# Three norms of a fused transformer kernel: who adds the eight squared chunks, VectorE or TensorE

## The reference, cut to what matters

```python
def rmsnorm(x, g):
    x32 = x.astype(jnp.float32)
    y = x32 * lax.rsqrt(jnp.mean(x32 * x32, axis=-1, keepdims=True) + RMS_EPS)
    return y.astype(x.dtype) * g

for i in range(DEPTH):
    h = h + 0.5 * swiglu(rmsnorm(h, ffn_norm_a[i]), ...)
    m = rmsnorm(h, mix_norm[i])
    h = h + mixer(m, ...)
    h = h + 0.5 * swiglu(rmsnorm(h, ffn_norm_b[i]), ...)
```

## Time and profile before

| what | before |
|---|---|
| median of 3 runs | 1870.84 us (1870.21 to 1872.37) |
| the profiled execution's own time | 1869.32 us |
| its span, first to last instruction | 1867.5 us |
| TensorE matmuls busy | 1738.5 us (93%) |
| VectorE busy | 1274.3 us (68%) |
| ScalarE busy | 910.5 us (49%) |
| GpSimd busy | 320.8 us (17%) |

### The profile page before, as it was taken

How to read it: one execution, slowest core, us unless ns; L and a number is a source line. 1 busy time by engine, 2 the same in 40 slices (tenths; PEclk the granted TensorE clock), 3 DMA queues, 4 the chain that set the end, 5 groups by cost and what they waited for, 6 DMA issues and landing times.

```text
span 1867.5 us, 29197 instructions
## 1 busy us (share of the span) xinstructions
PE 1738.5 (93%) x11150; PEld 1378.9 (74%) x11150; DVE 1274.3 (68%) x2524; ACT 910.5 (49%) x1905; POOL 320.8 (17%) x335
## 2 busy tenths in 40 slices
PE   9999999999999999999999999999987787877777
PEld 8999979999999999689999899975532222322222
DVE  6555787555765575876566887896777776766454
ACT  5344665444544453764444565635444444344433
POOL 1000004000000000030000000444333333333332
PEclk9999999999999999999999999999999999999999
DMA  8555426965465545225555444699999999999998
GB/s 300 190 183 188 146 85 161 271 251 187 158 201 184 187 154 184 80 93 188 195 175 176 150 137 137 222 406 422 421 421 422 421 421 422 421 421 422 421 422 318
DMA packets 96138, 483.70 MB, mean 259 GB/s; under 512 B 10576, under 2 KB 10832, under 8 KB 63360
## 3 DMA queue, kind: packets, MB, share of 16 engines
q0 software_dynamic: 38976, 275.25, 38.2%
q1 hardware_dynamic: 57024, 206.59, 32.9%
HBM read 477.34 MB, written 4.46 MB: 258 GB/s over the span
## 4 chain that ended last, share of the span: by engine, by line
PE 59%; DMA 16%; DVE 10%; issue 8%; POOL 4%; ACT 3%; POOLq 0%; SPq 0%; ACTq 0%; DVEq 0%
PE PS L562 15%; PE PS L564 15%; PE PS L563 15%; PE PS L2412 5%; DMA raw<-uv,A 5%; DMA WL<-uv,A 3%; DVE WL L1098 2%; DMA XL<-uv,A 2%; DMA A<-uv,A 2%; DMA raw<-wst 2%; PE PS L2448 1%; ACT WH L717 1%; DMA XF<-uv,A 1%; DMA YL<-uv,A 1%; POOL raw L695 1%
## 5 line engine op out<-in xcount | busy, mean ns | idle before, releaser
L1098 DVE TENSOR_TENSOR WL<-raw,WH 128x1024 fp32r<-128x1024 f32 (+2 forms) x372 | 447.9, 1245 | 76.8 <-ACT WH L717 76.5
L562 PE MATMUL PS<-XH,WH 128*128 128x256 f32 x1608 | 456.3, 284 | 4.7 <-DVE XL L1106 3.1
L563 PE MATMUL PS<-XL,WH 128*128 128x256 f32 x1608 | 452.5, 281 | 0.0
L564 PE MATMUL PS<-XH,WL 128*128 128x256 f32 x1608 | 452.4, 281 | 0.0
L717 ACT ACTIVATE WH<-raw 128x1024 fp32r<-128x1024 f32 (+2 forms) x372 | 369.2, 1042 | 41.0 <-PE PS L564 20.1
L562 PEld LDWEIGHTS PS<-XH,WH 128*128 128x128 f32 x1608 | 303.3, 189 | 9.3 <-DVE WL L1098 4.2
L563 PEld LDWEIGHTS PS<-XL,WH 128*128 128x128 f32 x1608 | 303.4, 189 | 0.1
L564 PEld LDWEIGHTS PS<-XH,WL 128*128 128x128 f32 x1608 | 303.3, 189 | 0.0
L1038 ACT ACTIVATE A<-A,RTK 128x1 f32<-128x1 f32 x256 | 74.9, 293 | 288.0 <-DVE A L1812 286.6
L772 ACT ACTIVATE A<-A 128x256 f32<-128x256 f32 x88 | 36.8, 418 | 342.7 <-DVE A L1140 342.7
L562 PE MATMUL PS<-GH,WH 128*128 128x256 f32 x704 | 198.3, 282 | 1.7 <-DVE WL L1098 1.1
(11 more groups left out here) (363 smaller groups left out, 2921.2 us busy)
## 6 DMA issues: line engine op xcount, KB each, us to landing
raw<-wst SPq DMA_DIRECT2D x378, 512.0 KB, 4.5
vscr<-A POOLq DMA_DIRECT2D x1, 3072.0 KB, 37.2
raw<-wst SPq DMA_DIRECT2D x6, 384.0 KB, 3.4
A<-vscr POOLq DMA_DIRECT2D x1, 2048.0 KB, 22.4
C<-cst SPq DMA_DIRECT2D x1, 1236.5 KB, 10.5
raw<-uv,A POOLq DMA_INDIRECT x66, 19.6
hT<-xin SPq DMA_DIRECT2D x2, 512.0 KB, 5.8
A<-vscr POOLq DMA_DIRECT2D x1, 1024.0 KB, 11.7
```

The source lines that it names most:

```text
L562: pe.matmul(o, wh, xh, start=start, stop=False, skip_group_check=True)
L563: pe.matmul(o, wh, xl, start=False, stop=False, skip_group_check=True)
L564: return pe.matmul(o, wl, xh, start=False, stop=stop, skip_group_check=True)
L1098: dv.tensor_tensor(WL[:, m % SPL, 0:w], raw[:, i % RAW, 0:w], f32(WH[:, m % SPL, 0:w]), ALU.subtract).then_inc(s_lo, 1)
```

## The change

At p = 1, 3 and 4 VectorE adds nothing any more; TensorE multiplies all eight squared chunks by ones, as it does at p = 0, and waits for ScalarE's semaphore of each square instead of VectorE's. p = 6 is as before. The table `SQ0` counts how often `s_sq` has been raised before each norm; it follows.

```diff
-        SQ0 = [sum(8 if q in (0, 6) else 2 if q in IN_PAIRS else 1 for q in range(p)) for p in range(9)]
+        SQ0 = [sum(8 if q in (0, 6) else 0 if q in IN_PAIRS else 1 for q in range(p)) for p in range(9)]
...
                 for i in range(4):
                     dv.wait_ge(s_sqr, 8 * IN_PAIRS.index(p) + 2 * i + 2)
-                    ins = dv.tensor_tensor(SQ[:, 2 * i, :], SQ[:, 2 * i, :], SQ[:, 2 * i + 1, :], ALU.add)
-                    if p == 6:
-                        ins.then_inc(s_sq, 1)
-                        continue
-                    own(ins)
-                    if i % 2:
-                        own.wait()
-                        dv.tensor_tensor(SQ[:, 2 * i - 2, :], SQ[:, 2 * i - 2, :], SQ[:, 2 * i, :], ALU.add).then_inc(s_sq, 1)
+                    dv.tensor_tensor(SQ[:, 2 * i, :], SQ[:, 2 * i, :], SQ[:, 2 * i + 1, :], ALU.add).then_inc(s_sq, 1)
...
                 if p == 6:
                     lo("qa", 2, 0)
-                pairs(p)
                 if p == 6:
+                    pairs(p)
                     lo("qa", 3, 0)
...
-                n = 8 if p == 0 else 4 if p == 6 else 2 if p in IN_PAIRS else 1
+                n = 4 if p == 6 else 8 if p == 0 or p in IN_PAIRS else 1
                 for i in range(n):
-                    pe.wait_ge(s_sq, SQ0[p] + i + 1)
-                    ins = pe.matmul(PS[:, 7, 0:T], c("ones"), SQ[:, i if n == 8 else 8 // n * i, :], start=i == 0, stop=i == n - 1, skip_group_check=True)
+                    if n == 8 and p:
+                        pe.wait_ge(s_sqr, 8 * IN_PAIRS.index(p) + i + 1)
+                    else:
+                        pe.wait_ge(s_sq, SQ0[p] + i + 1)
+                    ins = pe.matmul(PS[:, 7, 0:T], c("ones"), SQ[:, i if n == 8 else 2 * i, :], start=i == 0, stop=i == n - 1, skip_group_check=True)
```

## The result

| | before | after |
|---|---|---|
| median of 13 runs each | 1870.84 us | 1875.38 us |
| ratio of the changed kernel to the one before | | 1.0026 (95% interval 1.0019 to 1.0033) |
| span of the profiled execution | 1867.5 us | 1872.8 us |
| VectorE busy | 1274.3 us | 1268.6 us |
| TensorE's records of ones at `sums` | 42 | 78 |

The changed kernel is slower by 4.5 us in the median; by the ratio it is 0.26%, and its interval is 3.6 to 6.2 us. VectorE lost 18 instructions, 5.7 us of its busy time, and the program is no faster for it. One execution of a kernel further down, with p = 0 rounded, took 4321 us and counts in no ratio.

What follows compares the result with a forecast made beforehand. TensorE's own 1.80 us stretch at each place, not VectorE's adds, was taken as the bound. 1.77 + 0.92 + 1.77 = 4.46 us on the median 1870.84 gave 1875.3 us, range 1873.0 to 1876.8 us.

Steps and rivals of the forecast that it cites:

- The price of the products: At each place, sixteen float32 records take 3.57 us to the second matmul behind them, 0.216 us a record.
- The rival's price: At the three places, ones run at the plain 0.12 us a record: no change, 1870.7 us; chance 4%.
- The rule of the Trainium skill: For TensorE's warm matmuls, N ÷ 2.4 + 2.5 ns, 109 ns for 256 columns; sixteen records about 1.7 us.
- The stretch that is replaced: At each place, TensorE's 1.80 us from first product by ones to next unit's second matmul becomes 3.57, costing 1.77 us.
- The chain of waits: VectorE's adds on the chain around p = 3; rival that they set TensorE's stretch: 1867.8 us, faster, chance 1%.
- What came back at p = 3: At p = 3, TensorE's 0.85 us wait for first hidden values goes, so the place costs 0.92 us.
- The timing of `GL` taken over from p = 0: At p = 3, `GL` ends 8.46 us after the first product by ones, at 509.21 us, 0.67 before TensorE.
- What was left alone: At p = 1 and p = 4 nothing is taken back, though VectorE waits for TensorE soon after: 1.77 us each.
- The rival that weights come late anyway: In `ffn(1)`, a weight transfer stays put and TensorE waits 1.7 us less: +2.8 us, 1873.6 us; chance 14%.
- A sign that missed: Over the kernel, six adds fewer at each of three places leave VectorE busy 7.6 us less.

Runs made afterwards that it cites:

- the rounded kernel: Against the changed kernel, squares and ones at p = 1, 3 and 4 held in the split products' rounded format: 1867.81 us, ratio 0.9985 to the kernel before.
- The kernel without adds: Against the changed kernel, TensorE multiplies only two chunks by ones at the three places, six of eight left out: 1866.43 us, ratio 0.9976 to the kernel before.
- p = 0 rounded but not p = 6: Against the kernel before, squares and ones rounded at p = 0, 1, 3 and 4, p = 6 in plain float32: 1867.33 us, ratio 0.9980.

## Why the prediction was right

**The price of the products.** 3.57 us for a stretch with sixteen records, taken from p = 0 and p = 6, was measured three times out of three. The rival's price, 0.12 us a record, was measured as well, but only in the rounded kernel. The rule of the Trainium skill that was weighed, page "TensorE: Matmul & The Clock Gate", section "Back-to-back issue gap", gives 109 ns for 256 columns, and gives it for a single, isolated matmul. That comes near the rounded records (120 ns) and not the float32 records (216 ns); the measurement decides for these. So the rival that float32 ones run at the plain pace falls.

**The stretch that is replaced.** Counting the waits for the second sum and for low weights inside the 1.80 us, and the adds not at all, is what made the sum come out. The kernel without adds shows what they were worth there, 0.82 us; the one that keeps them shows that behind sixteen records they are worth nothing. The chain of waits was no lie: VectorE did come last by a little. But it doesn't say how close the next one is: TensorE was held up by 0.8 us, not by the 2.3 that the adds fill on the chain.

**What came back at p = 3.** 0.85 us were expected and 0.85 came: p = 3 costs 0.91 to 0.92 us in the kernels that give it sixteen records, and the wait stands in the one that doesn't. The timing of `GL` taken over from p = 0, 8.46 us after the first record, was measured as 510.93 − 502.46 = 8.47 us.

**What was left alone.** Nothing came back at p = 1 and p = 4, +1.77 and +1.79 us. The rival that weights come late anyway falls: the long transfer of the earlier trace rows moved with the program. The chain of the changed kernel, and TensorE's waits from 340 to 362 us:

```profile
320.20 27.19 DMA raw<-wst
```
```profile
PE PS L562 <- DVE WL L1098: 1.5, 2, 1.1
```

It is issued 1.91 us later than before (0.14 of it stood already at the first record of ones of p = 1), lands after about as long (27.19 us in place of 27.38), and TensorE loses 1.5 us to it in place of 1.7. Had it stood still, nearly all of that wait would have gone.

**The size.** 4.46 us were forecast, 4.54 measured in the medians, 4.48 in the three stretches. That the sum lands so close has some luck in it: the interval of the ratio is 3.6 to 6.2 us, a single stretch can be 1.5 us longer by the clock alone, and the medians of before moved between 1870.34 and 1871.43 us from one comparison to the next.

**A sign that missed.** VectorE was to be busy 7.6 us less and was 5.7 us less. VectorE's timeline before the change at p = 3, two pairs and the three low weights behind the adds:

```profile
498.79 0.75 DVE L1113 TENSOR_TENSOR A<-A 128x256 f32<-128x256 f32 x2
...
501.05 3.49 DVE L1098 TENSOR_TENSOR WL<-raw,WH 128x1024 fp32r<-128x1024 f32 x3
```

The 7.6 us add up durations, but neighbours overlap in the profile: two pairs of 0.42 us take 0.75 together, and by busy time all the adds were 6.8 us. The low weights ran close together before and stand apart now, 1.22 and 2.36 us in place of 3.49, so they count for more. Nothing in the sum of the forecast rests on the 7.6.

## What to carry to other kernels

A group of operations on the chain of waits is worth the distance to whoever comes next, not its own length; read the other engine's timeline at that place, from the first operation that changes to the first that doesn't, and replace the whole stretch. If the operation that is added already stands somewhere else in the kernel, take the stretch around it as a template, with the chain that follows, and ask in which format it runs: the same eight products by ones cost a stretch of 3.57 us in float32 and of 1.08 us in the rounded format. Before shortening a stretch, look at who is waited for right behind it: at p = 6 2.4 us of the 2.49 saved went straight into the next wait.

## What the runs showed of the hardware

TensorE's granted clock falls to its lower level for a short while in some executions, at places with small products, and not in others that have the same products there. The window 740 to 750 us of the sparse attention's compression in the changed kernel, and then in the one with the adds kept (span, then busy time and count of TensorE, its loads, VectorE, ScalarE and GpSimd, granted clock, DMA share, GB/s):

```profile
740.00:750.00 10.00, 10.00 (x86) 9.81 (x86) 3.86 (x6) 4.58 (x7) 0.00 (x0) 1.00 0.22 79
```
```profile
740.00:750.00 10.00, 10.00 (x73) 9.82 (x73) 3.95 (x6) 3.05 (x6) 0.00 (x0) 0.83 0.23 84
```

In the second, TensorE's timeline has 32 products of 30 columns just before, and then full products 0.21 us apart:

```profile
738.52 3.86 PE L2141 MATMUL PS<-A 128*128 128x30 f32 x32
...
742.77 0.41 PE L564 MATMUL PS<-XH,WL 128*128 128x256 f32 x1
742.98 0.41 PE L562 MATMUL PS<-XH,WH 128*128 128x256 f32 x1
```

The changed kernel has the same 32 products, from 738.87 us on, and the full ones behind them are 0.12 us apart.

And the kernel without adds, behind the products of one column at p = 1, in its timed run's profile:

```profile
216.00:220.00 4.00, 4.00 (x35) 3.87 (x34) 2.02 (x5) 1.99 (x4) 0.00 (x0) 1.00 0.85 299
220.00:222.00 2.00, 2.00 (x17) 1.99 (x18) 0.80 (x3) 0.00 (x0) 0.00 (x0) 0.96 0.39 145
222.00:224.00 2.00, 2.00 (x7) 1.65 (x7) 1.61 (x6) 0.27 (x1) 0.00 (x0) 0.50 0.00 0
224.00:226.00 2.00, 2.00 (x14) 2.00 (x14) 0.94 (x2) 1.41 (x4) 0.00 (x0) 0.69 0.69 254
```

From 222 to 224 us the granted clock is 0.50, the lower level of 1.2 GHz; just before, TensorE ran at full clock and had gone from full products to products of one column. With the fall from 740 us on, the stretch from p = 4 to p = 6 took 343.43 us where the changed kernel took 341.89: 1.5 us, a third of the whole effect under study. This fall, between 734 and 742 us, was also seen with p = 1 and 4 changed, with p = 0 rounded but not p = 6, and in one of the two executions of the kernel without adds; the other of the two, the changed kernel and the five other executions don't have it. So it doesn't go with one edit. The fall behind p = 1 was in both executions of the kernel without adds and in no other; whether the missing adds bring it isn't shown. Why a fall comes in one execution and not in the next stays open here. For small effects, a stretch is only to be compared between executions whose granted clock is the same in it.
